# Eight-slot rotation of expert panels, four experts per loop body, and identity products in the mixers of a two-block network on one core

## The reference, cut to what matters

```python
def moe(h, router_w, router_b, w_up, b_up, w_down, b_down):
    logits = xt @ router_w + router_b                 # 256 tokens, 32 experts
    top_vals, top_idx = lax.top_k(logits, 4)
    gates = jax.nn.softmax(top_vals, axis=-1)
    ...
    def expert_block(args):                           # the tokens that chose expert e
        hcat = xblk @ w_up[e] + b_up[e]               # w_up[e]: 1024 x 2048
        x_glu = jnp.minimum(hcat[:, 0::2], 7.0)
        x_lin = jnp.clip(hcat[:, 1::2], -7.0, 7.0)
        act = x_glu * jax.nn.sigmoid(1.702 * x_glu) * (x_lin + 1.0)
        return act @ w_down[e] + b_down[e]            # w_down[e]: 1024 x 1024
    ...
    return sum over the four chosen experts of gate * output
```

## Time and profile before

| | us |
|---|---|
| median of 3 runs | 1829.5 (1828.54 to 1830.59) |
| the profiled execution, its own time | 1827.99 |
| its span, first to last instruction | 1826.8 |
| TensorE (PE) busy | 1714.1 (94%) |
| VectorE busy | 806.8 (44%) |
| ScalarE busy | 607.2 (33%) |
| mean granted TensorE clock | 0.987 |

### The profile page before, as it was taken

One profiled execution on the slowest core, in us unless ns is written; L12 is line 12 of the kernel. 1 busy time (PEld: TensorE's weight loads), 2 busy tenths in 40 slices (PEclk: granted clock), 3 DMA queues, 4 the chain that ended last, 5 costly groups with the idle time before them and its releaser, 6 DMA issues.

```text
span 1826.8 us, 24748 instructions
## 1 busy us (share of the span) xinstructions
PE 1714.1 (94%) x9476; PEld 1037.7 (57%) x9477; DVE 806.8 (44%) x1141; ACT 607.2 (33%) x791; POOL 40.9 (2%) x77
## 2 busy tenths in 40 slices
PE   8999999889999999999999999989999998999996
PEld 8899997678999898877333332333323232333332
DVE  7854447744444657877332232222222222232234
ACT  6755445443555456653121121111111111121111
POOL 3000001000000110000000000000000000000000
PEclk9999999999999999999999999999999998999998
DMA  9535554502555444347799999999999998999995
GB/s 312 185 139 187 187 193 173 179 6 93 180 188 185 152 177 139 107 151 299 291 425 429 428 428 429 428 429 428 429 428 429 428 429 337 409 426 430 429 427 215
DMA packets 88229, 537.25 MB, mean 294 GB/s; under 512 B 10880, under 2 KB 13032, under 8 KB 63592
## 3 DMA queue, kind: packets, MB, share of 16 engines
q1 hardware_dynamic: 82568, 533.23, 72.5%
q10 hardware_dynamic: 5600, 3.15, 0.7%
HBM read 535.31 MB, written 1.05 MB: 294 GB/s over the span
## 4 chain that ended last, share of the span: by engine, by line
PE 60%; DMA 25%; DVE 8%; ACT 3%; issue 2%; ACTq 1%; PEldq 0%; SPq 0%; DVEq 0%
DMA expert_ring<-in_expert_w_up 25%; PE psA L2160 20%; PE psA L531 13%; PE psB L491 12%; PE psB L514 4%; PE psA L514 2%; PE psB L502 2%; DVE w_low L461 2%; PE psA L2166 1%; PE psB L382 1%; PE psB L1534 1%; PE psB L2189 1%; PE psA L2151 1%; ACT w_high L454 1%; PE psA L1179 1%
## 5 line engine op out<-in xcount | busy, mean ns | idle before, releaser
L2160 PE MATMUL psA<-expert_ring,gathered_T 128*64 128x512 f32 x1024 | 457.3, 599 | 30.7 <-DMA expert_ring<-in_expert_w_up 30.1
L2161 PE MATMUL psA<-expert_ring,gathered_T 128*64 128x512 f32 x1024 | 457.3, 599 | 0.0
L461 DVE TENSOR_TENSOR w_low<-panel_ring,w_high 128x1024 fp32r<-128x1024 f32 x244 | 296.1, 1222 | 204.1 <-ACT w_high L454 203.3
L454 ACT ACTIVATE w_high<-panel_ring 128x1024 fp32r<-128x1024 f32 x244 | 254.5, 1055 | 268.6 <-PE psA L531 111.5
L2160 PEld LDWEIGHTS psA<-expert_ring,gathered_T 128*64 128x64 f32 x1024 | 135.6, 138 | 344.4 <-issue 283.5
L2160 PE MATMUL psA<-expert_ring,activated_T 128*64 128x512 f32 x512 | 233.4, 598 | 2.2
L2161 PE MATMUL psA<-expert_ring,activated_T 128*64 128x512 f32 x512 | 233.4, 598 | 0.0
L491 PE MATMUL psB<-hT_high,w_high 128*128 128x256 f32 x712 | 202.3, 284 | 0.0
L491 PE MATMUL psB<-hT_high,w_low 128*128 128x256 f32 x712 | 201.5, 283 | 0.0
L491 PE MATMUL psB<-hT_low,w_high 128*128 128x256 f32 x712 | 201.5, 283 | 0.0
L2665 DVE TENSOR_SCALAR normed<-psA 128x512 f32<-128x512 f32 x32 | 22.1, 691 | 391.4 <-PE psA L2161 391.4
(11 more groups left out here) (468 smaller groups left out, 2466.9 us busy)
## 6 DMA issues: line engine op xcount, KB each, us to landing
expert_ring<-in_expert_w_up SPq DMA_DIRECT2D x128, 2048.0 KB, 25.4
expert_ring<-in_expert_w_down SPq DMA_DIRECT2D x64, 2048.0 KB, 22.2
panel_ring<-in_mlp_w SPq DMA_DIRECT2D x32, 2048.0 KB, 7.8
panel_ring<-in_w_in SPq DMA_DIRECT2D x11, 2048.0 KB, 7.9
panel_ring<-in_fox_w_in SPq DMA_DIRECT2D x6, 2048.0 KB, 8.5
panel_ring<-in_lru_w_in SPq DMA_DIRECT2D x3, 2048.0 KB, 13.2
panel_ring<-in_lru_w_out SPq DMA_DIRECT2D x2, 2048.0 KB, 16.3
panel_ring<-in_fox_w_out SPq DMA_DIRECT2D x2, 2048.0 KB, 8.0
```

The lines of the kernel that those rows point to most:

```text
L454: A.activation(part_rows(k.w[n % BUFFERS][0], view), view, ACT.Copy).then_inc(s.w_high, 1)
L461: V.tensor_tensor(w[1], view, w[0].bitcast(F32), ALU.subtract).then_inc(s.w_low, 1)
L2160: M.matmul(ps[0:SLOTS], lhsT, rhs[0], **flags)
L2161: return M.matmul(ps[SLOTS:P], lhsT, rhs[1], **flags)
```

## The change

Three edits. (1) The slot of panel j of expert e is the next one in a fixed rotation of all eight slots, so each load waits for the eighth panel ahead of it, of whatever kind. (2) As six panels per expert and eight slots come round together after four experts, the loop bodies of TensorE and SyncE now have four experts written out, and run eight times. (3) `stay_busy` becomes a function of its own, and is called seven times more in the mixers, with 12 identity products in all; the number of columns can be given. The two calls in `moe_pe` remain as they are.

```diff
+def stay_busy(k, out, n, columns=512):
+    for _ in range(n):
+        k.nc.tensor.matmul(out[:, 0:columns], k.ident[:], k.ident[:].unsqueeze(1).to_broadcast([P, columns // P, P]),
+                           start=True, stop=True)
...
     for j in (4, 5):
         project(j)
+    stay_busy(k, k.psA[:, 2, :], 4)
     for g in range(4):
         M.wait_ge(s.qk_normed, 2)
...
         transpose_pe(k, f.nat[g // 2], 4 * (g % 2), 4, k.psB[g % 2], k.ident[:])
+    stay_busy(k, k.psA[:, 2, :], 1)
     M.wait_ge(s.nat_evicted, 4)
...
             last.then_inc(s.scores, 1)
+        else:
+            stay_busy(k, k.psA[:, 0, :], 1, 384)
         if g >= 2:
...
         if 1 <= g <= PAIRS:
             ps, sc = k.psB[(g - 1) % 2], f.score[(g - 1) % 2]
+            if g == PAIRS:
+                stay_busy(k, k.psA[:, 0, :], 1)
             M.wait_ge(s.softmaxed, g)
...
+    stay_busy(k, k.psA[:, 0, :], 1, 256)
     M.wait_ge(s.values_read, PAIRS)
     for g in range(2):
         transpose_pe(k, f.nat[0], 4 * g, 4, k.psB[g], k.ident[:])
+    stay_busy(k, k.psA[:, 0, :], 1, 256)
     M.wait_ge(s.scores_read, PAIRS)
...
         if n == 0:
+            stay_busy(k, Z[:, 3, :], 2)
             M.wait_ge(s.o_sb_ready, 2)
...
-EXPERT_SLOTS = ((1, 2, 3, 4, 5, 6), (7, 0, 3, 4, 5, 6))
+SLOT_ORDER = (1, 2, 3, 4, 5, 6, 7, 0)
+FOUR = 4
+def expert_slot(i, j):
+    return SLOT_ORDER[(6 * i + j) % 8]
...
-    def expert(e, odd, pair):
+    def expert(e, at, four):
         def panel_in(j):
-            rounds = pair * 2 + odd if j >= 2 else pair
-            M.wait_ge(s.expert_in[EXPERT_SLOTS[odd][j]], rounds * 16 + 16)
+            M.wait_ge(s.expert_in[expert_slot(at, j)], four * (3 * 16) + (6 * at + j) // 8 * 16 + 16)
...
-    with M.Fori(0, NE // 2) as pair:
-        for odd in range(2):
-            expert(pair * 2 + odd, odd, pair)
+    with M.Fori(0, NE // FOUR) as four:
+        for at in range(FOUR):
+            expert(four * FOUR + at, at, four)
...
     def expert_slot_free(e, j):
-        n = e * 6 + (j - 5 if j >= 2 else j - 11)
+        n = e * 6 + (j - 7)
         S.wait_ge(s.released, n)
         S.sem_inc(s.settled, 1)
         S.wait_ge(s.consumed, n + COUNTED)
...
-    for j in range(2, 6):
-        expert_slot_free(1, j)
-        load(1, 1, j)
-    with S.Fori(1, NE // 2) as pair:
-        for odd in range(2):
+    for n in range(8, 6 * FOUR):
+        expert_slot_free(n // 6, n % 6)
+        load(n // 6, n // 6, n % 6)
+    with S.Fori(1, NE // FOUR) as four:
+        for i in range(FOUR):
             for j in range(6):
-                expert_slot_free(pair * 2 + odd, j)
+                expert_slot_free(four * FOUR + i, j)
                 S.sem_inc(s.settled, 1)
-                load(pair * 2 + odd, odd, j)
+                load(four * FOUR + i, i, j)
```

More of the change, by code:

```diff
@@ L1962, in __init__, with expert_panel @@
         self.actT_x, self.AT_x = self.actT[:, 0:2, :], self.at4[:, 0:2, :]
-EXPERT_SLOTS = ((1, 2, 3, 4, 5, 6), (7, 0, 3, 4, 5, 6))
-def expert_panel(k, odd, j):
-    return k.experts[:, EXPERT_SLOTS[odd][j], :].rearrange("p (k n) -> p k n", k=2 if j < 4 else 4)
+SLOT_ORDER = (1, 2, 3, 4, 5, 6, 7, 0)
+FOUR = 4
+def expert_slot(i, j):
+    return SLOT_ORDER[(6 * i + j) % 8]
+def expert_panel(k, i, j):
+    return k.experts[:, expert_slot(i, j), :].rearrange("p (k n) -> p k n", k=2 if j < 4 else 4)
 COUNTED = 1
@@ L2166, in up_bias, with up_panel @@
             M.matmul(m.U[half, c % 2, :], m.brow_of[rows, :], m.brow[rows, :], start=True, stop=False)
-    def up_panel(odd, j):
-        panel = expert_panel(k, odd, j)
+    def up_panel(at, j):
+        panel = expert_panel(k, at, j)
         for r in range(2):
@@ L2175, in up_panel, with down_panel @@
         return last
-    def down_panel(odd, j):
-        panel = expert_panel(k, odd, 4 + j)
+    def down_panel(at, j):
+        panel = expert_panel(k, at, 4 + j)
         for r in range(4):
@@ L2222, in extra_up_bias, with extra_up_panel @@
             M.matmul(m.U_x[quarter(q)], m.brow_x[quarter(q), :], m.brow_by4[quarter(q), :], start=True, stop=False)
-    def extra_up_panel(odd, j):
-        panel = expert_panel(k, odd, j)
+    def extra_up_panel(at, j):
+        panel = expert_panel(k, at, j)
         for r in range(2):
@@ L2235, in extra_transpose_activated, with extra_down_panel @@
         return last
-    def extra_down_panel(odd, j):
-        panel = expert_panel(k, odd, 4 + j)
+    def extra_down_panel(at, j):
+        panel = expert_panel(k, at, 4 + j)
         for r in range(4):
@@ L2250, in extra_scatter_tile @@
         return last
-    def stay_busy(ps, n):
-        for _ in range(n):
-            M.matmul(ps, k.ident[:], k.ident[:].unsqueeze(1).to_broadcast([P, 4, P]), start=True, stop=True)
     W = k.psA
@@ L2269, in moe_pe @@
     router_T_pe(k, 1)
-    stay_busy(W[:, 1, :], 1)
+    stay_busy(k, W[:, 1, :], 1)
     logits(1)
@@ L2284, in moe_pe @@
     M.matmul(W[:, 3, 0:NE], k.ones[:], m.sel[:, 1], start=False, stop=True).then_inc(s.placed, 1)
-    stay_busy(m.XR, 1)
+    stay_busy(k, m.XR, 1)
     for event in (s.act_T, s.gated_T, s.scattered, s.extra_pe, s.consumed):
@@ L2312, in first_half @@
                 panel_in(j)
-                up_panel(odd, j).then_inc(s.consumed, 1)
+                up_panel(at, j).then_inc(s.consumed, 1)
             panel_in(3)
-            up_panel(odd, 3).then_inc(s.consumed, 1)
+            up_panel(at, 3).then_inc(s.consumed, 1)
         def rest():
@@ L2333, in rest @@
             panel_in(4)
-            down_panel(odd, 0).then_inc(s.consumed, 1)
+            down_panel(at, 0).then_inc(s.consumed, 1)
             M.wait_ge(s.summed, 2 + e * 2)
@@ L2337, in rest @@
             panel_in(5)
-            down_panel(odd, 1).then_inc(s.consumed, 1)
+            down_panel(at, 1).then_inc(s.consumed, 1)
         tokens = nc.values_load(m.cnt[0:1, bass.ds(e, 1)], min_val=0, max_val=T, engines=[M.engine])
@@ L2359, in extra_up @@
             for j in range(4):
-                extra_up_panel(odd, j).then_inc(s.extra_pe, 1)
+                extra_up_panel(at, j).then_inc(s.extra_pe, 1)
         def extra_down(i):
@@ L2375, in extra_down @@
             for j in range(2):
-                extra_down_panel(odd, j).then_inc(s.extra_pe, 1)
+                extra_down_panel(at, j).then_inc(s.extra_pe, 1)
             M.wait_ge(s.summed, 3 + e * 2)
@@ L2744, in moe_sp, with load @@
     w_up, w_down = k.a["expert_w_up_2"][0], k.a["expert_w_down_2"][0]
-    def load(e, odd, j):
+    def load(e, i, j):
         at = slice(e, e + 1) if isinstance(e, int) else bass.ds(e, 1)
```

4 lines of the change are left out of this document (2 added, 2 removed).

## The result

The change makes the kernel 4.5% slower: 1914.63 us (1905.36 to 1915.71, four runs) against 1829.02 us (1827.43 to 1830.59, four runs) on the same chip, a ratio of 1.0452 with a 95% interval of 1.0436 to 1.0469. The forecast was 1860 us, its range 1824 to 1890. The sign was right, and so was the cause (the code is fetched anew); the size was not. The profiled execution took 1914.09 us, with a span of 1912.9.

What follows compares the result with a forecast made beforehand. Loads bound most experts before; refetched code was to make TensorE the bound. Missed branches inside experts and branches back, set against the profiled segments, gave +32.9, mixers -2: +31 on 1827.99, so 1859, median 1860 us; range 1824 to 1890.

Steps and rivals of the forecast that it cites:

- The code doesn't stay: TensorE's expert loop: the 205 KB four-expert body is fetched anew each round, each branch missing its target; +32.9 us together.
- first-contact price of expert 1: Expert 1's first branch over the extra code: 6,234 ns with loads at full rate, against 208 ns normally.
- The missed branch inside an expert: TensorE's branch over the extra code: a 2.15 us stall, 1.85 us net, making an expert 29.02 us instead of 27.17.
- The branch back: End of TensorE's loop body: a miss costs 0.7 to 3.6 us; 2.15 taken seven times, +15 us.
- The rotation worth nothing in this regime: Expert loads: with TensorE the bound, panels wait for it, so the rotation's 14.3 us gain is worth nothing.
- 8.5 + 2: Gains in us: 8.5 from the load stream starting earlier at the experts' start, 2 from the mixers' identity products.
- the 14.3: Rotation's worth in us if loads lead: 8.5 from the earlier start plus 5.8 behind expert 21.
- Loads pay for fetches: Expert loads: fifteen 16 KB packets per four experts at 428 GB/s add 0.14 us to the loads' 29.37 an expert.
- Mixers: Identity products in the mixers keep the clock at 1.00 from 408 to 418 us: -2 us, bounds -3.5 and +1.
- worse misses: Rival: packet crossings in TensorE's loop also come late, one more 1.85 us stall per expert, +59, above 1890; chance 0.07.

Runs made afterwards that it cites:

- The dead code: 512 never-executed instructions added to each of the two copies of the extra code, against the kernel before: 1844.93 us, ratio 1.0083.
- the plain body: Changed kernel with a four-expert body without extra code ahead of the full one in TensorE's loop, loop at a packet's start: 1843.22 us, ratio 1.0077 to the kernel before.
- the mixers' products: The mixers' identity products alone added to the kernel before, two-expert body kept: 1836.96 us over ten runs, ratio 1.0035 of nine.
- the hinted kernel: Changed kernel with hints for both long branches, the branch back's early, and TensorE's loop at a packet's start: 1826.27 us, ratio 0.9980 to the kernel before.

## Why the prediction was right in sign and short in size

**The code doesn't stay: right.** The branches take 6.06 us at the median, the first-contact price of expert 1. The reason given, a body of 205 KB, was too coarse. The dead code shows that 168 KB stay, and the plain body that 275 KB do, when a round needs eight packets, those fetched ahead included; the mixers' products show that 103 KB don't always stay when it needs nine. (The eight and the nine are counted in the compiled program; a trace shows only the packets that are fetched.) A round of the change fetches some fourteen, 99 in seven rounds. The Trainium skill, "Advanced Engine Details and Errata", section ISA Cache, gives TensorE 128 KB in lines of 16 KB, which is eight; the runs agree with the eight, if they are counted over what is executed and fetched ahead. That they are not counted over the body is shown.

**The missed branch inside an expert: right.** Expected +1.85 us net, seen 28.7 - 27.17 = 1.5, with a stall of 1.96 (forecast 2.15).

**The branch back: this term failed.** The step read "so I take the middle, 2.15, seven times", 15 us. Seven first experts took 262.7 us together, 59.6 more than seven of 29.02; 45 us of the missing 55 are here. The stall is 3.3 to 3.7 us, once 5.0, at the upper bound of 3.6 that the step had; it took the loads as nearly at rest, and while the first five of these branches waited they ran at 365 to 417 GB/s. The 1.0 us at the next packet's edge was costed at nothing ("the crossings ... were hidden in the first pass"), and it hangs on the 63 instructions that the head leaves in its packet. And 5.1 us are the clock (3.4 in the last of the seven).

**The clock: not priced at all.** TensorE that stands loses clock behind the stall. It fell in all seven first experts of a round for 7 to 10 us, and in eleven others for some 3.4 us; those took 30.7 us on average instead of 28.7. Against their forecast (29.02, and 31.93 for expert 22) these eleven are 16 us too long, and the other twelve that are neither the first of a round nor number 21 some 4 us shorter. With expert 0 shorter by 1.3 than forecast and expert 21 longer by 0.2, this and the 45 make the 55. The four-expert kernel with the hinted branch back shows that the stall is the cause: where it is cut to 1.2 to 2.4 us the 10 us drops are gone.

**The rotation worth nothing in this regime: too kind.** It brought nothing, and cost some 9 us (1.0411 against 1.0359), as its loads ran on beside the fetches. Where the code stays it was worth what the forecast has: 10.8 us were measured with the mixers, in a kernel without the stretch around expert 21, for which 8.5 + 2 were forecast. The other 5.8 of the 14.3 no run shows by itself. Its first issue came even earlier than foreseen (forecast 877.5, 884.37 before):

```profile
874.49 3.76 SPq L2768 DMA_DIRECT2D expert_ring<-in_expert_w_up  x2
```

**Loads pay for fetches: too small.** The forecast was 0.14 us an expert. In the hinted kernel, where it decides, it was 0.56 on average (29.93 against 29.37), in steps of 1.5. That is one reason why a kernel whose TensorE no longer waits for instructions there gains 0.2% only.

**Mixers:** forecast -2. The clock from 408 to 418 us is 1.00 as forecast, expert 0 ends 1.4 us earlier, with the stall in it that the forecast has for it (1.91 us). What was not seen is that 48 instructions ahead of the loop move its head.

The rival "worse misses", priced at one more stall of 1.85 us per expert and above 1890, is where the time came out. It named late crossings; of those there was only one a round. Its chance of 0.07 was too low, because a stall was priced as a stall alone.

## What to carry to other kernels

Before a loop's body is unrolled, count the packets of instructions that one round executes and those fetched behind each stretch, not the body's length: by that count eight stay here, and nine don't always. If it must be more, hint each long branch by more than the 6 us of a fetch ahead of it (13.7 worked and 0.9 didn't; nothing between was tried) and start the loop at a packet's start; if it is just eight, fix the head's place, since any edit ahead of the loop moves it. And price a stall of TensorE with the clock that it loses behind it: here 3.4 and 1.0 us of standing cost 8.9. Last, loads that are made to run without a pause also run beside the fetches, and make them longer.

## What the hardware showed unexpectedly

- A kernel whose loop needs nine packets is unsteady: nine of ten runs from 1825 to 1848 us, where the kernel before has 1828 to 1833, with three of 16 branches back missed in the profiled run.
- A fetch while the loads run takes 6 us, so a hint 13.7 us ahead of its branch works (1.07 us at the median) and one 0.9 us ahead doesn't (6.29 us). A hint at the loop's head brought the branch back of the long body from 6.14 to 1.12 us.
- 34 packets, 0.56 MB, went with 0.56 us more per expert for loads of 12.6 MB each, nearly five times what their bytes take at 428 GB/s (3.1 packets of 16 KB an expert, 0.12 us), and not evenly: fourteen panels land 4.9 us apart, the fifteenth 6.4.
- A missed branch took 3.9 to 5.2 us with the loads at 276 to 305 GB/s, and 5.8 to 6.1 with the loads at 423 to 438.
- The clock falls to 0.50 for 3.4 us behind many stalls of 2 us. In the five kernels with seven missed branches back each (stalls of 3.3 to 5.4 us) the first expert of a round has it for 6.8 or 10.2 us in 26 of 35 cases, and for 3.4 in the other nine.
